# Activation halves of a split fp32r matmul on other start addresses than the weights

## The reference

```python
# first block
h = modulate(rms_norm(x, norm1_w), sh1, sc1)
p = h @ w_in                                   # q, k, v, z, a, beta, short conv, gates: 9232 columns
o = gated_delta_rule_chunked(q, k, v, g, beta) # 8 heads of 128, chunks
y_a = (rms_norm(o) * silu(z)) @ w_gdn_proj
y_b = (gb * conv(gc * xin)) @ w_sc_out
x = x + g1 * ((gate_a * y_a + gate_b * y_b) @ w_o)
x = x + g2 * swiglu(modulate(rms_norm(x, norm2_w), sh2, sc2))   # 1024 -> 2 x 2816 -> 1024
x = modulate(rms_norm(x, normf_w), shf, scf)
# second block, two layers
h = x + pool_mixer(norm(x)); h = h + conv_ffn(norm(h))           # 1024 -> 2 x 2816 -> 1024
h = h + diff_attention(norm(h)); h = h + conv_ffn(norm(h))       # 8 heads
return norm(h)
```

## Time and profile before

| what | value |
|---|---|
| time before, median of 2 runs | 2199.72 us (2199.26 to 2200.18) |
| the profiled execution's own time | 2199.53 us |
| its span, first to last instruction | 2197.4 us |
| TensorE busy | 2140.6 us, 97% |
| VectorE, ScalarE, GpSimd busy | 1318.6, 858.9, 440.9 us |
| granted TensorE clock, mean | 0.99 of full speed |
| matmuls | 10504 |
| moved by DMA | 216.96 MB, mean 99 GB/s |

### The profile page before, as it was taken

The page is one execution under the profiler, slowest core; times in us unless marked ns, Lnnn a source line. Parts: engine busy times, 40 slices in busy tenths (PEclk is TensorE's granted clock), DMA queues, the critical chain, the costliest instruction groups (busy, mean ns, idle before and its releaser), DMA issues.

```text
span 2197.4 us, 30260 instructions
## 1 busy us (share of the span) xinstructions
PE 2140.6 (97%) x10504; PEld 1771.5 (81%) x10504; DVE 1318.6 (60%) x1881; ACT 858.9 (39%) x1352; POOL 440.9 (20%) x336
## 2 busy tenths in 40 slices
PE   6999999999999989999999999999999999999998
PEld 4788888888888878888888888888777777888887
DVE  6777777777644453443557655634788867555431
ACT  3333333333232233222335544432566635545322
POOL 0556765557610210000110000011000000000021
PEclk8999999999999999999999999999999999999999
DMA  7334333343323323333331333333122122333232
GB/s 288 106 104 124 107 103 105 105 124 110 99 82 120 113 80 96 95 95 91 96 122 57 101 99 97 91 98 98 58 58 58 53 82 86 96 95 95 89 99 72
DMA packets 394817, 216.96 MB, mean 99 GB/s; under 512 B 7881, under 2 KB 391299, under 8 KB 393220
## 3 DMA queue, kind: packets, MB, share of 16 engines
q1 hardware_dynamic: 393939, 213.64, 32.9%
q0 software_dynamic: 288, 2.10, 0.3%
q10 hardware_dynamic: 528, 0.40, 0.1%
HBM read 211.92 MB, written 4.19 MB: 98 GB/s over the span
## 4 chain that ended last, share of the span: by engine, by line
PE 85%; DVE 9%; ACT 2%; issue 2%; DMA 1%; SPq 1%; POOL 0%; POOLq 0%; ACTq 0%; DVEq 0%
PE ps L2143 25%; PE ps L2145 25%; PE ps L2144 25%; PE ps L2316 5%; PE ps L2170 2%; DVE small L2025 1%; DVE a_sb L2058 1%; DVE w_lo L1271 1%; DMA ada<-w_ada 1%; DVE a_t_lo L2034 1%; ACT at_swap L1162 1%; DVE prob L2053 1%; ACT prob L1185 0%; PE ps L2615 0%; PE ps L2383 0%
## 5 line engine op out<-in xcount | busy, mean ns | idle before, releaser
L2143 PE MATMUL ps<-h_hi,w_hi 128*128 128x512 f32 x1896 | 770.5, 406 | 7.1 <-DVE h_lo L1335 5.5
L2145 PE MATMUL ps<-h_hi,w_lo 128*128 128x512 f32 x1896 | 744.2, 393 | 0.0
L2144 PE MATMUL ps<-h_lo,w_hi 128*128 128x512 f32 x1896 | 741.8, 391 | 0.0
L1271 DVE TENSOR_TENSOR w_lo<-raw,w_hi 128x1024 fp32r<-128x1024 f32 x331 | 428.5, 1295 | 354.3 <-ACT w_hi L780 353.9
L780 ACT ACTIVATE w_hi<-raw 128x1024 fp32r<-128x1024 f32 x336 | 355.4, 1058 | 625.0 <-PE ps L2145 586.3
L2143 PEld LDWEIGHTS ps<-h_hi,w_hi 128*128 128x128 f32 x1896 | 359.0, 189 | 78.4 <-issue 13.8
L2145 PEld LDWEIGHTS ps<-h_hi,w_lo 128*128 128x128 f32 x1896 | 357.6, 189 | 78.2
L2144 PEld LDWEIGHTS ps<-h_lo,w_hi 128*128 128x128 f32 x1896 | 359.6, 190 | 65.1
L2143 PE MATMUL ps<-act_hi,w_hi 128*128 128x512 f32 x528 | 206.0, 390 | 0.0
L2145 PE MATMUL ps<-act_hi,w_lo 128*128 128x512 f32 x528 | 205.5, 389 | 0.0
L2144 PE MATMUL ps<-act_lo,w_hi 128*128 128x512 f32 x528 | 205.4, 389 | 0.0
(11 more groups left out here) (374 smaller groups left out, 2716.3 us busy)
## 6 DMA issues: line engine op xcount, KB each, us to landing
raw<-ffn_w_up SPq DMA_DIRECT2D x88, 512.0 KB, 3.7
raw<-w_in SPq DMA_DIRECT2D x72, 512.0 KB, 3.7
raw<-w_ffn_in SPq DMA_DIRECT2D x44, 512.0 KB, 3.7
ada_w<-w_ada SPq DMA_DIRECT2D x32, 512.0 KB, 3.9
raw<-ffn_w_down SPq DMA_DIRECT2D x32, 512.0 KB, 3.5
raw<-diff_w_qkv SPq DMA_DIRECT2D x24, 512.0 KB, 3.6
ada<-w_ada SPq DMA_DIRECT2D x8, 1024.0 KB, 12.5
ada_w<-w_ada_f SPq DMA_DIRECT2D x16, 512.0 KB, 3.8
```

What stands on the lines that cost most here:

```text
L1271: nc.vector.tensor_tensor(w_lo[:, tile.slot], raw[:, tile.raw], w_hi[:, tile.slot].bitcast(F32), SUB)\
L2143: nc.tensor.matmul(dst, w_hi[:, tile.slot, k], hi, start=first, stop=False)
L2144: nc.tensor.matmul(dst, w_hi[:, tile.slot, k], lo, start=False, stop=False)
L2145: return nc.tensor.matmul(dst, w_lo[:, tile.slot, k], hi, start=False, stop=last)
```

## The change

Only addresses change. The high and low tiles of h, og, sc and act start 32 to 224 bytes past a multiple of 256: h_hi at 192 and h_lo at 32, og_hi at 32 and og_lo at 224, sc_hi at 32 and sc_lo at 64, act_hi at 96 and act_lo at 160. raw, w_hi, w_lo and x stay where they are. Rows within a tile are 2048 bytes apart, so the distance is the same for every k. What follows a moved tile moves with it: cst now stands 32 bytes past a multiple of 256, masks, vec and state 64, shg 32; o_tok shares h_hi's place and its 192; sc_out and ga_t have 224, yb 64; work is rounded up to 256 only. The og group is placed behind the modulation tiles instead of from the end of SBUF. ao_hi, ao_lo and the tiles of the attention heads are placed from `wide` as before and stay on multiples of 256. The instructions on every engine and their order are the same.

```diff
@@ -302,8 +302,10 @@
         w_hi = sb("w_hi", [P, RING, KD, P], F32R)
         w_lo = sb("w_lo", [P, RING, KD, P], F32R)
         x = sb("x", [P, KD, T])
-        h_hi_at = place[0]
+        o_tok_at = place[0]
+        place[0] = o_tok_at + 192
         h_hi = sb("h_hi", [P, KD, T], F32R)
+        place[0] = o_tok_at + 4 * KD * T + 288
         h_lo = sb("h_lo", [P, KD, T], F32R)
@@ -319,12 +321,12 @@
-        work = place[0] = (place[0] + 511) // 512 * 512
+        work = place[0] = (place[0] + 255) // 256 * 256
...
-        end = nc.sbuf_usable_end // 512 * 512
+        end = nc.sbuf_usable_end // 8 * 8
@@ -339,10 +341,11 @@
-        og_hi = sb("og_hi", [P, H, T], F32R, at=end - 65536)
-        og_lo = sb("og_lo", [P, H, T], F32R, at=end - 49152)
-        sc_out = sb("sc_out", [P, KD, T], at=end - 32768)
-        ga_t = sb("ga_t", [P, KD, T], at=end - 16384)
+        og_at = work + 2048 * 17 + 8192 + 3072
+        og_hi = sb("og_hi", [P, H, T], F32R, at=og_at + 32)
+        og_lo = sb("og_lo", [P, H, T], F32R, at=og_at + 16384 + 224)
+        sc_out = sb("sc_out", [P, KD, T], at=og_at + 32768 + 224)
+        ga_t = sb("ga_t", [P, KD, T], at=og_at + 49152 + 224)
@@ -350,16 +353,16 @@
-        sc_hi = sb("sc_hi", [P, KD, T], F32R, at=work)
-        sc_lo = sb("sc_lo", [P, KD, T], F32R, at=work + 16384)
+        sc_hi = sb("sc_hi", [P, KD, T], F32R, at=work + 32)
+        sc_lo = sb("sc_lo", [P, KD, T], F32R, at=work + 16384 + 64)
...
-        yb = sb("yb", [P, T], at=work + 32768)
+        yb = sb("yb", [P, T], at=work + 32768 + 64)
...
-        act_hi = sb("act_hi", [P, KF, T], F32R, at=wide)
-        act_lo = sb("act_lo", [P, KF, T], F32R, at=wide + 2048 * KF)
+        act_hi = sb("act_hi", [P, KF, T], F32R, at=wide + 96)
+        act_lo = sb("act_lo", [P, KF, T], F32R, at=wide + 2048 * KF + 160)
@@ -369,7 +372,7 @@
-        at.update({n: sb("at_" + n, [P, T], at=wide + 4096 * KF + 2048 * j) for j, n in enumerate(("cos", "sin"))})
+        at.update({n: sb("at_" + n, [P, T], at=wide + 4096 * KF + 256 + 2048 * j) for j, n in enumerate(("cos", "sin"))})
@@ -385,7 +388,7 @@
-        o_tok = sb("o_tok", [P, NC, D], at=h_hi_at)
+        o_tok = sb("o_tok", [P, NC, D], at=o_tok_at + 192)
```

More of the change, by code:

```diff
@@ L352, in block_kernel @@
         ada_s = sb("ada_s", [P, 6, P], at=work + 2048 * len(names) + 8192)
-        assert work + 2048 * len(names) + 8192 + 3072 <= end - 65536
-        sc_hi = sb("sc_hi", [P, KD, T], F32R, at=work)
-        sc_lo = sb("sc_lo", [P, KD, T], F32R, at=work + 16384)
+        assert work + 2048 * len(names) + 8192 + 3072 == og_at
+        sc_hi = sb("sc_hi", [P, KD, T], F32R, at=work + 32)
+        sc_lo = sb("sc_lo", [P, KD, T], F32R, at=work + 16384 + 64)
         gb_t = x
-        yb = sb("yb", [P, T], at=work + 32768)
-        act_hi = sb("act_hi", [P, KF, T], F32R, at=wide)
-        act_lo = sb("act_lo", [P, KF, T], F32R, at=wide + 2048 * KF)
+        yb = sb("yb", [P, T], at=work + 32768 + 64)
+        act_hi = sb("act_hi", [P, KF, T], F32R, at=wide + 96)
+        act_lo = sb("act_lo", [P, KF, T], F32R, at=wide + 2048 * KF + 160)
         bands = sb("bands", [P, NC, len(WINDOWS), BAND], at=wide)
```

## The result

| | before | after |
|---|---|---|
| median of 2 runs | 2199.72 us | 2224.74 us (2223.69 to 2225.78) |
| span of the profiled execution | 2197.4 us | 2221.6 us |
| that execution's own time | 2199.53 us | 2223.69 us |

The ratio is 1.0123, 95% interval 1.0106 to 1.0141. It answers to a time before of 2197.7 us, a little under the two runs of the table, whose medians alone give 1.0114; 27 later runs of the kernel before lie between 2194.03 and 2200.20 us. So the change costs some 25 us by the table and 27 by the ratio (23 to 31 over its interval), and 24.2 us between the two profiled executions. That is less than 2%, but it lies far outside what repeated runs differ by: a small, certain loss, where I had forecast no effect.

What follows compares the result with a forecast made beforehand. TensorE's matmul spacing, 226.7 ns for each of 7656 matmuls, was taken to bound the kernel. Matmuls, other readers and writers, and DMAs each counted 0, sum 0 us, so 2199 us was forecast, range 2098 to 2248.

Steps and rivals of the forecast that it cites:

- The bound: Whole kernel: TensorE, busy 2140.6 of 2197.4 us, bounds it by how fast one matmul follows the next, 226.7 ns.
- The loss of 13.3 ns at full clock and none at half clock: 512-column matmuls: 226.7 ns against 213.3 at 2.4 GHz, 426 at half clock; 13.3 ns is the most addresses can return.
- Part 1: Moved h, og, sc, act: 7656 matmuls stay at 226.7 ns, effect 0, ends -102 and +102 us.
- the one point against zero: Second pooling piece, words at other offsets: 118.2 ns spacing, 1.8 of 13.3 ns less, from addresses or a start-up.
- rival B: Long stretches: aligned start is the good phase, offset loses it; 2236 us, or 2302 at worst; beyond 232.5 ns chance 0.15.
- The Trainium skill's two read ports: TensorE: loading the next weights steals no bandwidth from the running matmul, so no address matters; effect 0.
- Part 2: VectorE and ScalarE accesses to moved tiles: no effect; 9 us only if 5% slowing half fell on waits.
- Part 3: DMAs: weights land as before, the eight output stores read o_tok 192 bytes off; 0 to 4.8 us, taken as 0.
- A: Matmul spacing: loss is a collision of equal offsets, any offset removes it; 2098 us, half 2149; chance 0.38.
- C: Stages of h, og, sc, act: offset acts for some pairs only; act alone at most 21 us; small C within 0.47.
- what would show it: Start distance at L2143 to L2145: 226.7 ns right, 213 to 221 A, above 232.5 rival B; ao stays at 226.7.
- no change or a small shift: Whole kernel: up to 5.8 ns per matmul either way, with C where small, 2155 to 2244 us; chance 0.47.

Runs made afterwards that it cites:

- e1: Bare-tile kernel, split matmuls only, 99 cases of start distances: 226.7 ns at (0, 0 | 0) and (32, 32 | 32), 233.3 ns at (32, 32 | 0).
- e7: Bare-tile sweep with tiles about as far apart as in the kernel, 64 pairs behind four and seven small matmuls: equal starts 226.67 ns, (160, 32) 235.6 or 230.7.
- e3: Bare-tile kernel, 52 cases varying high and low weight distances, columns, rows, bank, order and type: 512 columns 226.67 ns at (0, 0), 233.3 at (32, 32); bf16 215.8.
- e4: Kernel after with og, sc and act back on multiples of 256, so only h moved: 2215.06 us, ratio 1.0081.
- e5: Kernel after with h back on multiples of 256, so only og, sc and act moved: 2209.92 us, ratio 1.0055.
- e8: Kernel before with raw and both weight parts moved 32 bytes, every activation on multiples of 256: 2240.56 us, ratio 1.0204.
- e6: As e4, only h moved, but with h_hi at 160 instead of 192 and h_lo at 32: 2221.46 us, ratio 1.0118.

## Why the prediction was wrong

**The bound.** Right: TensorE's spacing sets the time, and all of the difference lies in it.

**The loss of 13.3 ns at full clock and none at half clock.** Right as a reading, also for moved tiles: 427 ns in the first pair of rows of the after timeline. But I looked to it mainly for what addresses could give back. The settled 226.7 ns turned out to be the best of all pairs tried.

**Part 1, 7656 matmuls at 226.7 ns again, effect 0.** This is the step that failed. It rested on three arguments.
- *The activation stream passes every distance modulo 256 in each matmul, so where it starts does nothing.* The step doesn't hold: e1 shows 226.7 against 233.3 ns for the same streams with a start 32 bytes apart. What passing leaves open is the order in time. With equal starts the distances are 226 or 227 ns to the end of each case; with unequal starts most run through a pattern such as 235, 241, 231 (e7). That with equal starts every matmul meets its weight loads in the same way is my reading of this, and no run shows the two reads themselves.
- *The pooling pieces of the earlier trace rows pay the same 13.3 ns with other addresses.* The number is right and proves nothing: they are 256 columns wide, and e3 shows that at this width the effect of an offset can have the other sign (120.0 at equal starts, 116.7 at 32). The 118.2 ns that I named as the one point against zero may have been the same sort of sign; no run singles it out.
- *h, act, sc and og lie at other places and are equally long.* They all stood on multiples of 512 with the weights. That shows that far offsets don't matter, which e4 confirms for the odd multiples of 256 (act at 226.75 ns there), and nothing about near ones.

In place of 226.7 ns the moved matmuls of the long stretches took 231.0 to 233.2 ns. The nearest row was the one I set aside: the earlier trace rows, 231.4 ns behind transposes, by which I had written 36 us for rival B. In size it was right, only its count was too high. That the uneven spacing behind transposes and the one of unequal starts are the same thing isn't shown, so the agreement may be luck. The 36 us take all 7656 matmuls from 226.7 to 231.4, but in the heads' stage, where runs of six follow transposes, the distance was 230.4 ns before and is 231.7 now: +1.2 us. What was left to lose with this pair lay in the long stretches. From the stages of e4 and e5: h +4.8 (w_o and feed-forward 1), +3.2 and +4.6 (feed-forwards 2 and 3), together 12.6 us; act 3.3 + 3.4 + 3.1 = 9.8 us; gates 2.1 us. That makes 24.5, with the heads' 1.2 us 25.7. The preparation stage took 1.4 us less, but it lies anywhere from 131.9 to 134.9 us in the seven full kernels, in no order that the addresses explain (it has 17.1 to 23.9 us at half clock, the most in the longest); with it the sum is 24.3, against a measured 24.2. Both hold the gain of 3.2 us by the clock, since e4 had half clock in feed-forwards 1 and 2 for as long as the kernel after.

**The Trainium skill's two read ports** (TensorE: Matmul & The Clock Gate, Step-by-step: what each phase is for): from them I drew that no address matters. For fp32r operands that doesn't hold, 226.7 against 228.9 to 235.6 ns, with the distance between weights and activations deciding; whether bandwidth is what is lost isn't shown. The three bf16 cases, 215.8 ns each, agree with it. The N/2.4 + 2.5 of the same page's section Back-to-back issue gap, 215.8 ns for 512 columns, is met by the bf16 stream of e3 to the tenth, and by no fp32r stream here.

**Part 2, other readers and writers.** Right. The same two forms of VectorE as in the earlier trace rows, after:

```profile
L1805 DVE SCALAR_TENSOR_TENSOR tmp<-tmp,vec 128x511 f32<-128x511 f32 x44 | 32.8, 746 | 0.4 <-issue 0.4
...
L2061 DVE SCALAR_TENSOR_TENSOR a_sb<-prob,small 128x512 f32<-128x512 f32 x32 | 24.1, 752 | 3.7 <-PE ps L2173 2.6
```

746 and 752 ns, against 745 and 752. Waits of engines beside the path grew, most of all ScalarE's for a free weight slot (586.3 us before, 609.8 now), as TensorE frees them more slowly; they cost nothing:

```profile
L783 ACT ACTIVATE w_hi<-raw 128x1024 fp32r<-128x1024 f32 x336 | 355.3, 1058 | 648.7 <-PE ps L2148 609.8
```

**Part 3, DMAs.** Right within its 0 to 4.8 us: the stores of the output take 2.9 us each instead of 2.7.

```profile
out<-o_tok SPq DMA_DIRECT2D x8, 256.0 KB, 2.9
```

**The rivals.** A (any offset removes the loss) is refuted: no unequal case fell below 226.7 ns at 512 columns. B happened, at its lower price and short of 232.5 ns in the mean. C happened inside it: every moved pair loses in the long stretches, but between 4.4 and 6.6 ns. In "what would show it" the sentence on ao was right (226.9), and so was the guess at what would make me wrong, only with the other sign: equal starts are special, as the good case. The measured time lies inside what I had called no change or a small shift (2155 to 2244 us), but that class was wide enough for either sign and says nothing for the mechanism; and the 44 us that I took for what can be told from no change were far too many, since 27 runs of the kernel before lie within 6.2 us. The likelihoods suffered from one thing above all: the change could move each matmul by -13.3 to +13.3 ns, and I took the middle for the likeliest, though the one row with an uneven spacing said +4.7.

**Still open.** What the remaining 13.3 ns at equal starts are. It isn't the bytes of the weight load, the PSUM bank, the order or the high and low parts (e1, e3); it is absent with bf16 operands and at half clock. Every case loads new weights for every matmul; none leaves the weight load out, so that the two reads get in each other's way is the likeliest cause, but argued and not shown. Why the sign can turn at 256 columns is open as well. Nor do these runs say why a case settles in one pattern or the other, or what holds at distances of 16 bytes. No version tried beats the kernel before.

## What to carry to other kernels

Where fp32r matmuls of 512 columns follow each other with a new weight tile each, place activations and weights at the same distance modulo 256; which multiple of 32 it is doesn't matter, and starting everything on multiples of 256 does it. That is shown for weight tiles of 128 columns. Long unbroken runs gain up to 6.6 ns for each 226.7 by it; in the short runs behind small matmuls (230.4 ns with equal starts) unequal ones cost 1.3 ns with the change's h, 2.4 in e8 and 3.8 in e6. Test the exact width before trusting it, since at 256 columns it was the other way round for three of four moved pairs. And when one row of the trace shows a worse value of the very quantity that a change may touch (here 231.4 ns), price it times the instructions that don't pay it yet, and don't take the middle of the bounds. Compare the clock of each stage too before adding up differences of single executions: here it hid some 3 of 27 us.

## What the runs showed of the hardware

- The distance between fp32r matmuls of 512 columns, with a new weight tile of 128 columns each, depends at full clock on start addresses: 226.67 ns when all operands have the same distance from a multiple of 256 (0, 32, 64, 96, 128, 160, 192, 224), 228.9 to 235.6 ns in all other pairs tried in steps of 32 bytes (e1, e7). At half clock it is 427 ns with equal and unequal starts.
- bf16 operands take 215.8 ns, with the activations at 0, 32 and 96 bytes and the weights at 0 (e3).
- A stream of matmuls at fixed addresses can settle in more than one pattern of distances, and what ran ahead of it decides which (235.6 or 231.1 ns for one pair, by the number of small matmuls). So a bare-tile sweep gives a range for a pair rather than its value in a kernel: in its long stretches e6 lost 231.1 - 226.7 = 4.4 ns where the sweep had said 8.9.
- At equal starts the extra time is no fixed number per matmul: 13.3 ns at 256, 320 and 384 columns, 20.0 at 448, 16.7 at 480 and 13.3 at 512. A start 32 bytes off adds 6.6 ns at 512 columns and 3.3 at 384 and 480, and takes 3.3 away at 256 (e3).
